# A layer with a mixer and a mixture of experts on one core: a tenth preloaded weight piece in the place of the residual's permuted copy, a strided first gather, and an end shared by ScalarE and VectorE

## The chip, the core and the metric

The kernel runs on one core of one Trainium2 chip. The metric is the device time of one execution in microseconds (us). Three runs of the kernel before have a median of 1313.36 us (1310.47 to 1313.62). The profile is of one further execution, which took 1310.38 us.

## What is computed

One layer over 256 tokens of width 2048, all in float32. First the mixer: an input projection, three token mixers, an output projection, and the residual sum. Then the experts:

```
x = x + y @ w_out                       # y: what the mixers give
h2 = rmsnorm(x, norm_ffn)
x = x + hierarchical_moe(h2, ...)       # 32 experts, 2 for each token
# in an expert:
hid = silu(xb @ w_gate[e]) * (xb @ w_up[e])     # 2048 -> 512
out = hid @ w_down[e]                           # 512 -> 2048
```

Every expert has weights of 12 MB (w_gate, w_up, w_down of 4 MB each), so the second part reads 384 MB from memory.

## The kernel before, in words

**Mixer part.** 29 weight pieces of 2 MB (21 of w_in, 8 of w_out) come through four ring buffers. ScalarE (L676) and VectorE (L989) split each into two parts, TensorE multiplies them (L1465, L1467). The last eight pieces give, in column blocks of 256, the residual sum `x_acc` (VectorE L1075, L1076), which the experts' part reads and adds to. After each block GpSimd copies it into `x2_perm` (L605, L606), in which the 128 elements that one matmul needs lie side by side; in `x_acc` they lie 16 elements (64 bytes) apart. Then come the router and the ranks of the tokens (VectorE L1202 to L1252), in which TensorE runs empty matmuls (`keep_clock`, L1407).

**Experts' part.** An expert is an item, four items are a quad, and there are eight quads. For a quad, `gather` (L1651 to L1665) multiplies the residual by a matrix of zeros and scaled ones: the residual's 128x128 chunk is the stationary operand, `pick` the moving one. There are 16 chunks for each of two token tiles, so 32 matmuls; in the first quad the first 16 stand ahead of the first item and the other 16 after its first two pieces. VectorE puts the result into `x_exp` (L1327). An item then takes its weights in six pieces of 2 MB: in the first quad in the order gate half, up half, gate half, up half (L1697), down half, down half (L1743). In between the gate and the up sums are folded over four row groups (`fold_part`, L1677: stationary `gate_sb` or `up_sb`, read 4 elements or 16 bytes apart; moving `fold`, 32 columns). After each piece TensorE raises `piece_used`. The results of an item are added to the residual while the next item runs: TensorE spreads them over the tokens (`combine`, L1647), VectorE adds (`accumulate`, L1337).

**The queue of weights.** SP issues all loads in one order. It waits for a buffer to be free, then issues. In the first quad it has eight ring buffers and one more, `starter`, for piece 8 (pieces are numbered 0 to 23 in the quad). So pieces 0 to 8 are issued with no regard to the experts' work: 0 and 1 once `y_parts` is split (`y_split`), 2 to 5 as the mixer's buffers come free (`lo_ready`), 6 to 8 as the mixer's last matmuls end (`quarter_used`). Piece 9 waits for the use of piece 0, piece 10 for that of piece 1, and so on (L451):

```
else:
    sp.wait_ge(piece_used, m - STARTER if m <= STARTER + MOE_RING else m - MOE_RING + 1)
```

From the second quad on, the same buffers are four pairs of 4 MB (`twin`), filled with a whole w_gate, w_up or w_down (L475), and the last two matrices of the last item come in halves again (L471).

**The end.** The last item has empty matmuls at two places, three ahead of the first down half and six ahead of the second (`keep_clock`). Then `combine` spreads its result: four matmuls for token tile 0 into four PSUM banks, four for tile 1 into the same banks, each of which waits until VectorE has read its bank. VectorE adds eight blocks of 512 columns (L1337), and SP writes each to memory as it is ready (L504, 256 KB each).

Of the kernel before, what the change touches and what calls it, by code (L numbers as in the profile page):

```python
# [23 lines left out]
F32 = mybir.dt.float32  # L24
# [13 lines left out]
def hymba_layer(nc, x, norm_mix, w_in, conv_a_w, conv_a_b, lru_wa, lru_ba, lru_wx, lru_bx, lru_lam,  # L38
# [54 lines left out]
    with ExitStack() as ctx:  # L93
# [43 lines left out]
        proj = at("proj", [BLK_V, SEQ], F32, o)  # L137
        x2_perm = at("x2_perm", [TILES, KC, P], F32, o)
# [79 lines left out]
        b_gath, b_up_fold, b_comb = [bank[4], bank[5]], bank[4], bank[4:8]  # L218

# [4 lines left out]
        starter_in = sem("starter_in")  # L224
# [40 lines left out]
        comb_full, acc_done = sem("comb_full"), sem("acc_done")  # L265
# [10 lines left out]
        STARTER = MOE_RING  # L276

        def slot_of(m):

            return m if m <= STARTER else (m - STARTER - 1) % MOE_RING  # L280

# [4 lines left out]
        def begun(m):  # L286
            return m == STARTER

# [16 lines left out]
        def half_landed(q, k, part, h):  # L305
# [5 lines left out]
            return q * (16 * PER_QUAD // MOE_RING) + 16 * ((3 * k + part) // (MOE_RING // 2) + 1  # L311
# [9 lines left out]
        def half_of(q, k, part, h):  # L321

            if first_quad(q):
                m = first_piece(k, part, h)
                return starter[:, :] if begun(m) else ring[MOE_ORDER[slot_of(m)]][:, :]
# [14 lines left out]

        def second_quad(q):
            return isinstance(q, int) and q == 1
# [42 lines left out]
        def _(sp):  # L385
# [48 lines left out]
            def quad(q, n_extra=None):  # L434
                def item_pieces(k, e):
                    for i in range(PARTS):
                        m = PARTS * k + i
                        if m < 2:
# [15 lines left out]
                        dst = starter if begun(m) else ring[place_of(k, i)]  # L454
                        sp.dma_start(dst[:, :].rearrange("p (c n) -> p c n", n=src.shape[2]),
                                     src).then_inc(starter_in if begun(m) else piece_in[place_of(k, i)], 16)

                def item_twins(k, e):
                    for part, whole in enumerate((w_gate_p, w_up_p, w_down_p)):
# [29 lines left out]
            quad(1)  # L489
            with sp.Fori(2, QUADS - 1) as q:  # L490
                quad(q)
# [17 lines left out]
        def _(pool):  # L509
# [91 lines left out]

            for k in range(N_OUT):
                pool.wait_ge(proj_free, N_IN + k + 1)
# [8 lines left out]
        def _(act):  # L612
# [289 lines left out]
            quad(QUADS - 1)  # L902
            act.wait_ge(table_ready, 1)
# [8 lines left out]
        def _(dve):  # L912
# [482 lines left out]
            with dve.If(n_extra > 0):  # L1395
                with dve.Fori(QUADS, QUADS + XQ) as q:
# [400 lines left out]
```

## Time and profile before

| | before |
|---|---|
| median of 3 runs | 1313.36 us (1310.47 to 1313.62) |
| profiled execution | 1310.38 us |
| its span | 1308.6 us |
| TensorE busy | 1129.7 us, 86% |
| VectorE busy | 510.0 us, 39% |
| ScalarE busy | 280.5 us, 21% |
| GpSimd busy | 57.3 us, 4% |
| read from memory | 468.83 MB |
| written to memory | 2.10 MB |

The span is the time from the first to the last recorded instruction; 1.8 us of the execution lie around it. Busy shares are means over stages with different limits. The mixer lasts until about 380 us, the router until 392, the experts until the end.

### The profile page before, as it was taken

What the parts mean: (1) busy time and instruction counts of PE and PEld (TensorE: products, weight loads), DVE (VectorE), ACT (ScalarE), POOL (GpSimd) and SP (SyncE); (2) the same over time, 40 slices, a digit from 0 to 9 for tenths busy, and PEclk for the clock granted to TensorE, in tenths of its full rate; (3) what the DMA queues carried; (4) which work ended last, traced back from release to release, by engine and by line L of the source; (5) the groups of instructions that cost most, each with busy time, mean ns of one, the idle gap of its engine ahead of it and who ended that gap; (6) DMA issues with size and microseconds to landing.
All of it is one profiled execution on the core that took longest, in us unless ns stands there. A gap on an engine that the chain in (4) does not pass through costs nothing.

```text
span 1308.6 us, 17772 instructions
## 1 busy us (share of the span) xinstructions
PE 1129.7 (86%) x7343; PEld 658.1 (50%) x7343; DVE 510.0 (39%) x817; ACT 280.5 (21%) x444; POOL 57.3 (4%) x72
## 2 busy tenths in 40 slices
PE   8999999999999988878787887987887797779677
PEld 7888888878885444324323323423242253234223
DVE  6646677775444353223222222322232232222223
ACT  7445576684430000000000000000000000000000
POOL 3000011501100000000000000000000000000000
PEclk9999999999999888888878978888788798888888
DMA  9955554746678999999999999999999999999996
GB/s 323 293 190 176 159 181 140 246 129 201 273 297 336 425 435 429 430 432 430 432 433 432 432 431 430 433 433 433 432 432 433 431 431 433 433 433 430 431 424 262
DMA packets 83856, 471.61 MB, mean 360 GB/s; under 512 B 7154, under 2 KB 68192, under 8 KB 69216
## 3 DMA queue, kind: packets, MB, share of 16 engines
q1 hardware_dynamic: 83808, 470.94, 88.2%
q8 instruction: 34, 0.56, 0.2%
q14 instruction: 14, 0.11, 0.0%
HBM read 468.83 MB, written 2.10 MB: 360 GB/s over the span
## 4 chain that ended last, share of the span: by engine, by line
PE 52%; DMA 40%; DVE 4%; ACT 1%; issue 1%; POOL 1%; DVEq 0%; SPq 0%; ACTq 0%
PE banks L1465 16%; DMA twin<-in_w_gate 15%; DMA twin<-in_w_up 15%; DMA twin<-in_w_down 10%; PE banks L1697 9%; PE banks L1467 8%; PE banks L1743 6%; PE banks L1677 3%; PE banks L1647 3%; PE banks L1663 3%; DVE x_acc L1337 2%; PE banks L1407 1%; PE banks L1486 1%; DVE up_sb L1350 1%; POOL h_tok L555 1%
## 5 line engine op out<-in xcount | busy, mean ns | idle before, releaser
L1697 PE MATMUL banks<-twin,x_exp 128*32 128x512 f32 x1760 | 252.5, 698 | 83.2 <-DMA twin<-in_w_gate 68.0
L1337 DVE TENSOR_TENSOR x_acc<-x_acc,banks 128x512 f32<-128x512 f32 x256 | 158.5, 682 | 343.5 <-PE banks L1647 343.4
L1465 PE MATMUL banks<-hT,w_split 128*128 128x512 f32 x576 | 203.9, 398 | 0.1
L989 DVE TENSOR_TENSOR w_split<-ring,w_split 128x1024 fp32r<-128x1024 f32 x116 | 146.7, 1284 | 112.6 <-ACT w_split L676 112.0
L1697 PEld LDWEIGHTS banks<-twin,x_exp 128*32 128x32 f32 x1760 | 50.0, 118 | 236.2 <-issue 131.7
L1467 PE MATMUL banks<-hT,w_split 128*128 128x256 f32 x576 | 161.2, 280 | 0.0
L1743 PE MATMUL banks<-twin,hidT 128*32 128x512 f32 x864 | 144.3, 829 | 19.3 <-DVE hidT L1356 9.7
L676 ACT ACTIVATE w_split<-ring 128x1024 fp32r<-128x1024 f32 x116 | 121.7, 1060 | 122.0 <-PE banks L1467 121.9
L1465 PEld LDWEIGHTS banks<-hT,w_split 128*128 128x128 f32 x576 | 108.0, 188 | 25.4 <-issue 0.3
L888 ACT ACTIVATE y_item<-banks 64x512 f32<-64x512 f32 x32 | 18.9, 591 | 472.4 <-PE banks L1743 472.4
L1467 PEld LDWEIGHTS banks<-hT,w_split 128*128 128x128 f32 x576 | 108.7, 189 | 0.2
L1677 PE MATMUL banks<-fold,up_sb 128*128 128x32 f32 x256 | 65.5, 399 | 42.4 <-DVE up_sb L1350 42.4
L1677 PEld LDWEIGHTS banks<-fold,up_sb 128*128 128x128 f32 x256 | 62.2, 327 | 72.2 <-DVE x_acc L1337 55.4
L1647 PE MATMUL banks<-y_item,give 32*128 32x512 f32 x512 | 93.8, 769 | 2.6 <-DVE x_acc L1337 1.8
L1361 DVE COPY y_item<-banks 64x512 f32<-64x512 f32 x32 | 22.2, 695 | 179.3 <-PE banks L1743 179.3
L1465 PE MATMUL banks<-w_split,y_parts 128*128 128x512 f32 x256 | 90.6, 398 | 0.5 <-DVE y_parts L1058 0.5
L1743 PEld LDWEIGHTS banks<-twin,hidT 128*32 128x32 f32 x864 | 34.6, 144 | 107.1 <-issue 92.8
L872 ACT ACTIVATE gate_sb<-banks 128x512 f32<-128x512 f32 x32 | 19.1, 597 | 305.1 <-PE banks L1697 305.1
L1677 PE MATMUL banks<-fold,gate_sb 128*128 128x32 f32 x256 | 65.7, 401 | 8.2 <-ACT gate_sb L872 8.2
L1467 PE MATMUL banks<-w_split,y_parts 128*128 128x256 f32 x256 | 71.4, 279 | 0.0
L1677 PEld LDWEIGHTS banks<-fold,gate_sb 128*128 128x128 f32 x256 | 62.1, 327 | 16.5 <-ACT gate_sb L872 15.9
L1647 PEld LDWEIGHTS banks<-y_item,give 32*128 32x128 f32 x512 | 27.4, 229 | 83.4 <-issue 79.1
(244 smaller groups left out, 925.9 us busy)
## 6 DMA issues: line engine op xcount, KB each, us to landing
twin<-in_w_gate SPq DMA_DIRECT2D x28, 4096.0 KB, 32.5
twin<-in_w_up SPq DMA_DIRECT2D x27, 4096.0 KB, 32.3
twin<-in_w_down SPq DMA_DIRECT2D x27, 4096.0 KB, 32.3
ring<-in_w_in SPq DMA_DIRECT2D x20, 2048.0 KB, 9.0
ring<-in_w_up SPq DMA_DIRECT2D x10, 2048.0 KB, 15.8
ring<-in_w_down SPq DMA_DIRECT2D x10, 2048.0 KB, 16.7
ring<-in_w_out SPq DMA_DIRECT2D x8, 2048.0 KB, 8.3
ring<-in_w_gate SPq DMA_DIRECT2D x7, 2048.0 KB, 11.8
```

Source lines behind the costliest of these rows:

```text
L676: act.activation(w_hi[:, k], src, ACT.Copy).then_inc(hi_ready, 1)
L872: act.activation(gate_sb[:, :], b_gate[:, :], ACT.Copy).then_inc(gate_out, 1)
L989: dve.tensor_tensor(w_lo[:, k], src, w_hi[:, k].bitcast(F32), ALU.subtract).then_inc(lo_ready, 1)
L1337: dve.tensor_tensor(dst, dst, b_comb[n][:, :], ALU.add).then_inc(acc_done, 1)
L1361: dve.tensor_copy(y_item[k % 2][P // 2:P, :], b_down[P // 2:P, :]).then_inc(y_out_dve, 1)
L1465: pe.matmul(dst[:, 0:2 * PW], stationary[:, 0, cols], moving.rearrange("p s n -> p (s n)"), start=(k == 0 and cc == 0), stop=False)
L1467: ins = pe.matmul(dst[:, PW:2 * PW], stationary[:, 1, cols], moving[:, 0, :], start=False, stop=(k == 3 and cc == 3))
L1647: pe.matmul(b_comb[n][:, :], give[par][rows, t, :], y_item[par][rows, :], start=True, stop=True).then_inc(comb_full, 1)
L1663: ins = pe.matmul(b_gath[b % 2][:, c * P:(c + 1) * P], x2_perm[:, t, 4 * b + c, :], pick[:, t].rearrange("p i s -> p (i s)"), start=(t == ...
L1677: ins = pe.matmul(to[:, f * SLOTS:(f + 1) * SLOTS], part[:, :].rearrange("p (k f) -> p f k", f=FC)[:, f, :], fold[:, :], start=True, stop= ...
L1697: ins = pe.matmul(dst[SLOTS * j:SLOTS * (j + 1), :], x_exp[:, c, cols], weights[:, cc * F:(cc + 1) * F], start=(c < 4), stop=(c >= KC - 4))
L1743: ins = pe.matmul(b_down[SLOTS * n:SLOTS * (n + 1), :], hidT[:, f, :], weights[:, ff * D + n * DB:ff * D + (n + 1) * DB], start=(f == 0), ...
```

## The change

- `starter2`, a buffer of 2 MB, is laid over `x2_perm`. It takes piece 2 of the first quad (the second gate half of the first expert), and SP issues it with pieces 0 and 1. The ring buffer that piece 2 had goes to piece 3, and so on, so that piece 9 has a buffer of its own, too. Pieces 0 to 9 are now issued ahead, and pieces 10 to 23 wait for `piece_used`.
- `x2_perm` can only be written when piece 2 has been used. GpSimd now makes its 16 copies then, in one go. VectorE waits for them ahead of its first addition to `x_acc`, and the second quad's gather waits for them.
- The first quad's gather reads `x_acc` itself, with its chunks' elements 64 bytes apart.
- SP's second quad is no longer written out; its waits follow the rule of the later ones.
- At the end, the empty matmuls give way to four matmuls that put blocks 1 and 3 of each token tile of the residual into PSUM (`residual_first`, stationary `ident`, 512 moving columns). The last combine uses eight banks and waits for none to be read; for blocks 1 and 3 it adds to what is there, and ScalarE copies the sum out. VectorE adds blocks 0 and 2 as before. The output goes in four writes of 512 KB, each after one addition and one copy.
- VectorE raises `acc_done` four times more where there are further items, which is a branch that this input doesn't take (no instruction of it is in the trace).

```diff
+        starter2 = at("starter2", [KC * PW], F32, o)
...
+        last_comb = [bank[4:8], [bank[3], bank[0], bank[1], bank[2]]]
...
-        STARTER = MOE_RING
+        STARTERS = (8, 2)
+        FIRST = MOE_RING + len(STARTERS)
         def slot_of(m):
-            return m if m <= STARTER else (m - STARTER - 1) % MOE_RING
+            if m >= FIRST:
+                return (m - FIRST) % MOE_RING
+            return m - len([e for e in STARTERS if e < m])
...
-        def slot_user(s):
-
-            return max(m for m in range(PER_QUAD) if not begun(m) and slot_of(m) == s)
+        def slot_user(s, upto=PER_QUAD):
+
+            return max(m for m in range(upto) if not begun(m) and slot_of(m) == s)
+
+        FIRST_PAIR = (PER_QUAD - FIRST) % MOE_RING // 2
         def twin_of(k, part):
-            return (3 * k + part) % (MOE_RING // 2)
+            return (3 * k + part + FIRST_PAIR) % (MOE_RING // 2)
...
+                        if m < 2 or begun(m) and begun_at(m) == 1:
                             sp.wait_ge(y_split, 4)
-                        elif m < 6:
-
-                            sp.wait_ge(lo_ready, 4 * (N_MIX - 6 + m) + 4)
-                        elif m == 6:
-
-                            sp.wait_ge(quarter_used, 4 * N_MIX - 2)
-                        elif m <= STARTER:
+                        elif begun(m):
                             sp.wait_ge(quarter_used, 4 * N_MIX)
+                        elif slot_of(m) < 6 and m < FIRST:
+
+                            sp.wait_ge(lo_ready, 4 * (N_MIX - 6 + slot_of(m)) + 4)
+                        elif m < FIRST:
+
+                            sp.wait_ge(quarter_used, 4 * N_MIX - 2 if slot_of(m) == 6 else 4 * N_MIX)
                         else:
-                            sp.wait_ge(piece_used, m - STARTER if m <= STARTER + MOE_RING else m - MOE_RING + 1)
+                            sp.wait_ge(piece_used, slot_user(slot_of(m), m) + 1)
...
-                        if second_quad(q) and 3 * k + part < 4:
-
-                            sp.wait_ge(piece_used, max(slot_user(2 * j), slot_user(2 * j + 1)) + 1)
-                        else:
-                            sp.wait_ge(piece_used, q * PER_QUAD + 2 * (3 * k + part) - 6)
+                        sp.wait_ge(piece_used, q * PER_QUAD + 2 * (3 * k + part) - 6)
...
-            quad(1)
-            with sp.Fori(2, QUADS - 1) as q:
+            with sp.Fori(1, QUADS - 1) as q:
...
-            for b in range(8):
-                t, n = b // 4, b % 4
+            for b in range(4):
+                t, d = b // 2, slice(b % 2 * 2 * DB, (b % 2 + 1) * 2 * DB)
                 sp.wait_ge(acc_done, (NE - 1) * 8 + (b + 1))
-                sp.dma_start(out_t[t][:, n * DB:(n + 1) * DB], x_acc[:, t, n * DB:(n + 1) * DB]).then_inc(out_done, 16)
-            sp.wait_ge(out_done, 16 * 8)
+                sp.wait_ge(acc_done_act, b + 1)
+                sp.dma_start(out_t[t][:, d], x_acc[:, t, d]).then_inc(out_done, 16)
+            sp.wait_ge(out_done, 16 * 4)
...
+            pool.wait_ge(piece_used, STARTERS[1] + 1)
             for k in range(N_OUT):
-                pool.wait_ge(proj_free, N_IN + k + 1)
...
             quad(QUADS - 1)
+
+            for b in range(4):
+                t, n = b // 2, b % 2 * 2 + 1
+                act.wait_ge(comb_full, (NE - 1) * 8 + (4 * t + n + 1))
+                act.activation(x_acc[:, t, n * DB:(n + 1) * DB], last_comb[t][n][:, :],
+                               ACT.Copy).then_inc(acc_done_act, 1)
...
+                if first_quad(q) and k == 1:
+
+                    dve.wait_ge(x2_perm_ready, N_OUT)
...
-            accumulate(NE - 1, 0)
-            accumulate(NE - 1, 1)
+            for b in range(4):
+                t, n = b // 2, b % 2 * 2
+                dve.wait_ge(comb_full, (NE - 1) * 8 + (4 * t + n + 1))
+                dst = x_acc[:, t, n * DB:(n + 1) * DB]
+                dve.tensor_tensor(dst, dst, last_comb[t][n][:, :], ALU.add).then_inc(acc_done, 1)
...
+            def residual_first(t, n):
+
+                pe.matmul(last_comb[t][n][:, :], ident[:, :], x_acc[:, t, n * DB:(n + 1) * DB], start=True, stop=False)
+
+            def last_combine(t):
+
+                outputs_written(NE)
+                pe.wait_ge(give_ready, NE)
+                for n in range(4):
+                    rows = slice(SLOTS * n, SLOTS * (n + 1))
+                    pe.matmul(last_comb[t][n][:, :], give[1][rows, t, :], y_item[1][rows, :],
+                              start=(n % 2 == 0), stop=True).then_inc(comb_full, 1)
...
-                if first_quad(q):
-                    pe.wait_ge(x2_perm_ready, N_OUT)
+                def x2_chunk(t, c):
+                    if first_quad(q):
+                        return x_acc[:, t, :].rearrange("p (k c) -> p c k", c=KC)[:, c, :]
+                    return x2_perm[:, t, c, :]
+
                 pe.wait_ge(pick_ready, q + 1)
                 if not first_quad(q):
+
+                    pe.wait_ge(x2_perm_ready, N_OUT)
...
-                            ins = pe.matmul(b_gath[b % 2][:, c * P:(c + 1) * P], x2_perm[:, t, 4 * b + c, :],
+                            ins = pe.matmul(b_gath[b % 2][:, c * P:(c + 1) * P], x2_chunk(t, 4 * b + c),
...
-                    keep_clock(b_up, 3)
+
+                    pe.wait_ge(acc_done, (NE - 1) * 8)
+                    for n in (1, 3):
+                        residual_first(0, n)
...
-                        keep_clock(b_up, 6)
+
+                        pe.wait_ge(give_ready, NE)
+                        for n in (1, 3):
+                            residual_first(1, n)
...
-            combine(NE - 1, 0, 1)
-            combine(NE - 1, 1, 1)
+            last_combine(0)
+            last_combine(1)
```

On the queue SP, in the first quad, the program before had these loads (the ring's number is behind the name; one row for each piece, from piece 0):

```order
L455 DMA ring6_56<-in_w_gate 128x4096 [waits y_split]
L455 DMA ring7_57<-in_w_up 128x4096 [waits y_split]
L455 DMA ring1_51<-in_w_gate 128x4096 [waits lo_ready]
L455 DMA ring2_52<-in_w_up 128x4096 [waits lo_ready]
L455 DMA ring3_53<-in_w_down 128x4096 [waits lo_ready]
L455 DMA ring0_50<-in_w_down 128x4096 [waits lo_ready]
L455 DMA ring4_54<-in_w_gate 128x4096 [waits quarter_used]
L455 DMA ring5_55<-in_w_up 128x4096 [waits quarter_used]
L455 DMA starter_76<-in_w_gate 128x4096 [waits quarter_used]
L455 DMA ring6_56<-in_w_up 128x4096 [waits piece_used]
```

and the changed one has these:

```order
L463 DMA ring6_56<-in_w_gate 128x4096 [waits y_split]
L463 DMA ring7_57<-in_w_up 128x4096 [waits y_split]
L463 DMA starter2_82<-in_w_gate 128x4096 [waits y_split]
L463 DMA ring1_51<-in_w_up 128x4096 [waits lo_ready]
L463 DMA ring2_52<-in_w_down 128x4096 [waits lo_ready]
L463 DMA ring3_53<-in_w_down 128x4096 [waits lo_ready]
L463 DMA ring0_50<-in_w_gate 128x4096 [waits lo_ready]
L463 DMA ring4_54<-in_w_up 128x4096 [waits quarter_used]
L463 DMA starter_76<-in_w_gate 128x4096 [waits quarter_used]
L463 DMA ring5_55<-in_w_up 128x4096 [waits quarter_used]
L463 DMA ring6_56<-in_w_down 128x4096 [waits piece_used]
```

Ten loads instead of nine stand ahead of the first that waits for the experts' work. Piece 2 moved from the third wait for `lo_ready` to that for `y_split`, and each of pieces 3 to 7 has taken the wait of the one before it.

On TensorE, from the last item's second fold to its last combine, the program before had (`y_item_77` and `give_78` are the last item's result and its table of gates):

```order
L1677 MATMUL banks<-fold,up_sb 128x32 x3
L1407 MATMUL banks<-ident 128x128 x3
L1743 MATMUL banks<-ring_54,hidT 32x512 [waits y_out_dve,piece_in4,y_out_act,hid_ready]
L1743 MATMUL banks<-ring_54,hidT 32x512 x7
L1407 MATMUL banks<-ident 128x128 x6
L1743 MATMUL banks<-ring_55,hidT 32x512 [waits piece_in5]
L1743 MATMUL banks<-ring_55,hidT 32x512 x7
L1647 MATMUL banks<-y_item_77,give_78 128x512 [waits give_ready,acc_done,y_out_dve,y_out_act]
L1647 MATMUL banks<-y_item_77,give_78 128x512 [waits acc_done] x3
```

and the changed one:

```order
L1715 MATMUL banks<-fold,up_sb 128x32 x3
L1659 MATMUL banks<-x_acc,ident 128x512 [waits acc_done]
L1659 MATMUL banks<-x_acc,ident 128x512
L1787 MATMUL banks<-ring_53,hidT 32x512 [waits y_out_dve,piece_in3,y_out_act,hid_ready]
L1787 MATMUL banks<-ring_53,hidT 32x512 x7
L1659 MATMUL banks<-x_acc,ident 128x512 [waits give_ready]
L1659 MATMUL banks<-x_acc,ident 128x512
L1787 MATMUL banks<-ring_50,hidT 32x512 [waits piece_in0]
L1787 MATMUL banks<-ring_50,hidT 32x512 x7
L1667 MATMUL banks<-y_item_77,give_78 128x512 [waits give_ready,y_out_dve,y_out_act]
L1667 MATMUL banks<-y_item_77,give_78 128x512 x3
```

Two wide matmuls stand where three narrow ones stood, and two where six stood, both ahead of a down half; the combine's wait for `acc_done` is gone.

## Rows read from the trace of the kernel before

**Rows 1.** The page: traffic in 40 equal slices, and the chain's shares.
```profile
GB/s 323 293 190 176 159 181 140 246 129 201 273 297 336 425 435 429 430 432 430 432 433 432 432 431 430 433 433 433 432 432 433 431 431 433 433 433 430 431 424 262
PE 52%; DMA 40%; DVE 4%; ACT 1%; issue 1%; POOL 1%; DVEq 0%; SPq 0%; ACTq 0%
```

**Rows 2.** Stretches: us, busy by engine (count), TensorE clock, DMA share, GB/s.
```profile
345.00:370.00 25.00, 25.00 (x148) 21.06 (x147) 12.75 (x13) 11.52 (x20) 2.29 (x4) 1.00 0.46 172
393.50:399.00 5.50, 5.50 (x53) 3.49 (x55) 1.65 (x4) 0.00 (x0) 0.00 (x0) 1.00 0.00 0
399.00:401.00 2.00, 2.00 (x21) 1.16 (x14) 0.00 (x0) 0.00 (x0) 0.00 (x0) 1.00 0.89 246
```

**Rows 3.** Timeline of SP's queue: start, us, instruction.
```profile
319.86 1.82 SPq L455 DMA_DIRECT2D ring<-in_w_gate  x1
...
379.26 0.43 SPq L455 DMA_DIRECT2D starter<-in_w_gate  x1
398.38 0.33 SPq L455 DMA_DIRECT2D ring<-in_w_up  x1
400.09 5.95 SPq L455 DMA_DIRECT2D ring<-in_w_down  x2
410.34 0.33 SPq L455 DMA_DIRECT2D ring<-in_w_gate  x1
415.58 0.33 SPq L455 DMA_DIRECT2D ring<-in_w_up  x1
417.30 0.33 SPq L455 DMA_DIRECT2D ring<-in_w_gate  x1
```

**Rows 4.** The chain in order of time, the first item: start, us, what.
```profile
392.89 3.57 PE banks L1663 x32
396.46 3.57 PE banks L1697 x32
400.03 3.77 PE banks L1663 x32
403.80 1.90 PE banks L1697 x16
```

**Rows 5.** Timeline: weight loads with contiguous, strided and contiguous stationary operands.
```profile
383.64 0.52 PEld L1606 LDWEIGHTS banks<-fold_halves,logitsT 128*128 128x128 f32 x4 [1.42 <-DVE logitsT L1157]
406.37 1.94 PEld L1677 LDWEIGHTS banks<-fold,gate_sb 128*128 128x128 f32 x8 [0.55 <-ACT gate_sb L872]
399.96 3.65 PEld L1663 LDWEIGHTS banks<-pick,x_perm 128*128 128x128 f32 x32 [0.84 <-issue]
```

**Rows 6.** Timeline: GpSimd's last pair of copies, and VectorE's first additions.
```profile
380.37 1.12 POOL L606 COPY x_perm<-x_acc 128x256 f32<-128x256 f32 x2 [8.94 <-DVE x_acc L1076]
422.76 4.87 DVE L1337 TENSOR_TENSOR x_acc<-x_acc,banks 128x512 f32<-128x512 f32 x8
```

**Rows 7.** The chain in order of time, the last item: start, us, what.
```profile
1240.22 33.50 DMA twin<-in_w_gate
1291.16 0.75 PE banks L1407 x6
1293.77 1.54 PE banks L1407 x12
1295.30 1.90 PE banks L1743 x16
```

**Rows 8.** Stretches at the end, columns as in group 2.
```profile
1300.50:1306.25 5.75, 2.37 (x8) 0.86 (x6) 3.52 (x6) 0.00 (x0) 0.00 (x0) 0.68 0.98 360
1306.25:1308.60 2.35, 0.00 (x0) 0.00 (x0) 0.00 (x0) 0.00 (x0) 0.00 (x0) 0.50 0.09 29
```

**Rows 9.** Timeline of the end: the last additions and the output's writes.
```profile
1299.15 4.87 DVE L1337 TENSOR_TENSOR x_acc<-x_acc,banks 128x512 f32<-128x512 f32 x8 [1.23 <-PE banks L1647]
1299.86 4.52 SPq L504 DMA_DIRECT2D out<-x_acc  x8
```

**Rows 10.** One line's instructions: ns min/median/max, and ScalarE's copy of 512 columns.
```profile
L872 ACT ACTIVATE gate_sb<-banks x32: 597/597/599, 405.7 to 1278.7; 128x512 f32<-128x512 f32 x32
```

More of the change, by code:

```diff
@@ L223, in hymba_layer @@
         piece_in = [sem(f"piece_in{i}") for i in range(MOE_RING)]
-        starter_in = sem("starter_in")
+        starter_in = [sem(f"starter_in{i}") for i in range(2)]
         consts_ready = sem("consts_ready")
@@ L264, in hymba_layer @@
         y_out_act, y_out_dve = sem("y_out_act"), sem("y_out_dve")
-        comb_full, acc_done = sem("comb_full"), sem("acc_done")
+        comb_full, acc_done, acc_done_act = sem("comb_full"), sem("acc_done"), sem("acc_done_act")
         gath_full, gath_out = sem("gath_full"), sem("gath_out")
@@ L286, in begun, with begun_at @@
         def begun(m):
-            return m == STARTER
+            return m in STARTERS
+        def begun_at(m):
+            return STARTERS.index(m)
         def uses_of(m):
             return len([e for e in range(m + 1) if not begun(e) and slot_of(e) == slot_of(m)])
-        def slot_user(s):
-            return max(m for m in range(PER_QUAD) if not begun(m) and slot_of(m) == s)
+        def slot_user(s, upto=PER_QUAD):
+            return max(m for m in range(upto) if not begun(m) and slot_of(m) == s)
+        FIRST_PAIR = (PER_QUAD - FIRST) % MOE_RING // 2
         def twin_of(k, part):
-            return (3 * k + part) % (MOE_RING // 2)
+            return (3 * k + part + FIRST_PAIR) % (MOE_RING // 2)
         def half_place(q, k, part, h):
@@ L310, in half_landed @@
                 return 16 * (uses_of(slot_user(s)) + 1 + MIX_USES[half_place(q, k, part, h)])
-            return q * (16 * PER_QUAD // MOE_RING) + 16 * ((3 * k + part) // (MOE_RING // 2) + 1
+            in_first = uses_of(slot_user(2 * twin_of(k, part))) - PER_QUAD // MOE_RING
+            return q * (16 * PER_QUAD // MOE_RING) + 16 * ((3 * k + part) // (MOE_RING // 2) + 1 + in_first
                                                            + MIX_USES[half_place(q, k, part, h)])
@@ L324, in half_of @@
                 m = first_piece(k, part, h)
-                return starter[:, :] if begun(m) else ring[MOE_ORDER[slot_of(m)]][:, :]
+                return (starter, starter2)[begun_at(m)][:, :] if begun(m) else ring[MOE_ORDER[slot_of(m)]][:, :]
             if apart(q, k, part):
@@ L339, in first_quad @@
             return isinstance(q, int) and q == 0
-        def second_quad(q):
-            return isinstance(q, int) and q == 1
         def closing_quad(q):
@@ L437, in item_pieces @@
                         m = PARTS * k + i
-                        if m < 2:
+                        if m < 2 or begun(m) and begun_at(m) == 1:
                             sp.wait_ge(y_split, 4)
-                        elif m < 6:
-                            sp.wait_ge(lo_ready, 4 * (N_MIX - 6 + m) + 4)
-                        elif m == 6:
-                            sp.wait_ge(quarter_used, 4 * N_MIX - 2)
-                        elif m <= STARTER:
+                        elif begun(m):
                             sp.wait_ge(quarter_used, 4 * N_MIX)
+                        elif slot_of(m) < 6 and m < FIRST:
+                            sp.wait_ge(lo_ready, 4 * (N_MIX - 6 + slot_of(m)) + 4)
+                        elif m < FIRST:
+                            sp.wait_ge(quarter_used, 4 * N_MIX - 2 if slot_of(m) == 6 else 4 * N_MIX)
                         else:
-                            sp.wait_ge(piece_used, m - STARTER if m <= STARTER + MOE_RING else m - MOE_RING + 1)
+                            sp.wait_ge(piece_used, slot_user(slot_of(m), m) + 1)
                         src = piece_source(i, e)
-                        dst = starter if begun(m) else ring[place_of(k, i)]
+                        dst = (starter, starter2)[begun_at(m)] if begun(m) else ring[place_of(k, i)]
                         sp.dma_start(dst[:, :].rearrange("p (c n) -> p c n", n=src.shape[2]),
-                                     src).then_inc(starter_in if begun(m) else piece_in[place_of(k, i)], 16)
+                                     src).then_inc(starter_in[begun_at(m)] if begun(m) else piece_in[place_of(k, i)], 16)
                 def item_twins(k, e):
@@ L1391, in _ @@
             quad(QUADS - 1)
-            accumulate(NE - 1, 0)
-            accumulate(NE - 1, 1)
+            for b in range(4):
[3 more added lines that the diff above has]
+                dve.tensor_tensor(dst, dst, last_comb[t][n][:, :], ALU.add).then_inc(acc_done, 1)
             n_extra = dve.value_load(tab[0:1, 0:1], min_val=0, max_val=NX - 1)
             with dve.If(n_extra > 0):
+                dve.wait_ge(acc_done_act, 4)
+                for b in range(4):
+                    dve.tensor_copy(lru_t[:, 0, b:b + 1], silu_sb[:, 0, 0:1]).then_inc(acc_done, 1)
                 with dve.Fori(QUADS, QUADS + XQ) as q:
@@ L1630, in landed @@
                     if begun(m):
-                        pe.wait_ge(starter_in, 16)
+                        pe.wait_ge(starter_in[begun_at(m)], 16)
                     else:
```

## The prediction

> **What bounds the kernel.** I began with the traffic over the whole span [rows 1]. From slice 15 to slice 39 it stands at 424 to 435 GB/s and never lower: once the experts run, the weights' stream is the bound. The last number, 262, and the numbers up to the 14th are lower: there something else holds the transfers back. The chain's shares say the same: 40% of it is DMA, and TensorE's 52% is mostly the mixer and the ends of items. So three places matter: when the stream starts without a hole, how many pieces it has left then, and what lies behind its last pieces.
>
> The start is seen in the stretches [rows 2]: nothing moves from 393.5 to 399.0 us, because all nine preloaded pieces have landed and the tenth waits for the first to be used. From 399 to 401 the queue moves 246 GB/s x 2 us = 0.49 MB, which at 431 GB/s takes 1.14 us, so the stream starts at about 399.86. SP issued at 398.38 [rows 3], so from issue to stream is 1.48 us. A piece of 2.097 MB takes 4.86 us at 431 GB/s. The chain in that time is TensorE alone: gather 3.57 us, two pieces 3.57, gather 3.77, third piece 1.90 [rows 4].
>
> **What the tenth piece gives.** One piece less is left at the start: at most 4.86 us. Loading it ahead costs nothing: SP issues it behind pieces 0 and 1, at about 322, 1.9 us and a load after the one at 319.86 [rows 3], and between 345 and 370 the DMA engines are idle 54% of the time [rows 2], 13.5 us. The mixer's last w_out piece was issued before them, so it isn't delayed.
>
> But less of it arrives. Before, the refills were issued when pieces 0 to 4 had been used: 398.38, 400.09, 405.71 (second of the pair at 400.09), 410.34, 415.58, then 417.30 [rows 3]. The stream needed them at 399.86 + 4.86 each: the third refill at 409.58, the fourth at 414.44, the fifth at 419.30. In the change the second gate half has no buffer to give back (its place becomes `x2_perm`), so the third refill waits for the fourth use: 410.34 + 1.48 = 411.82 instead of 409.58. The fourth waits for the fifth use: 415.58 + 1.48 = 417.06, where the stream is ready at 411.82 + 4.86 = 416.68. Before, this same data started at 419.30. With all else equal the stream is 2.2 us earlier, not 4.86. The later refills aren't late (417.30 + 1.48 against 421.92).
>
> **What the strided gather costs.** The first gather's stationary operand is now read with 64 bytes between elements. No row shows that stride, but one shows 16 bytes: the fold's eight loads of 128x128 take 1.94 us, 0.243 each [rows 5]. With the same number of partitions and 36 moving columns in place of 32, but a contiguous operand, four take 0.52 us, 0.130 each; the gather's own 32 take 3.65, 0.114 each [rows 5]. So a stride costs 0.113 to 0.129 us for a load; I take 0.12. A half of the gather has 32 loads (two for each float32 matmul): 3.8 us more. TensorE is the chain here [rows 4] and nothing covers it. Bounds: nothing extra if the fold were slow for another reason, and twice as much, 0.24 us, since 64 bytes are further than 16; I take the fold's value, because its elements too lie each in another 16 bytes.
>
> The Trainium skill (SBUF — State Buffer, Door 1, on SBUF cachelines) says that accesses within a 16-byte line run at full bandwidth and each crossing pays, and also that four fp32 are free to stride. The fold, at just four, pays, so the trace bears out the first half and not the second. By the first, 64 bytes would cost what 16 do.
>
> Uses 0 and 1 come 3.8 us later, use 3 and all after it 7.6. The fourth refill then starts at 415.58 + 7.6 + 1.48 = 424.66 (the third at 410.34 + 9.08 = 419.42, done at 424.28). Against 419.30 the stream is **5.4 us later**. The fifth, at 417.30 + 9.08 = 426.4, is in time for 429.5. From there on SP is ahead of the stream, and its one-piece-earlier waits in the second quad change nothing.
>
> **The copies on GpSimd.** They were behind other work before, so removing them from the mixer saves nothing. Now 16 of them start after use 2, at 405.71 + 7.6 = 413.3, and take 16 x 0.56 = 9 us at the pace of the last pair [rows 6], until 422.3. VectorE would wait for them at its first addition, 422.76 + 7.6 = 430.4 [rows 6]. Cover: 8 us; cost nothing. Without that cover, the second item's combine and fold would wait behind VectorE.
>
> **The end.** The last item hangs on its gate matrix, which lands at 1273.7 [rows 7]; from there TensorE, VectorE and ScalarE follow each other without another wait for a load. Three empty matmuls took 0.75 us and six 1.54 [rows 7]. A full-width pass of 512 columns costs what four quarter-width ones side by side do: 16 in 1.90 us [rows 7], four rounds, so 0.43 to 0.48 each, and two passes for each float32 matmul: 0.86 to 0.95. Two matmuls are 1.7 to 1.9 us. Both groups stand ahead of a down half, so the last down half ends 1.0 + 0.2 = 1.2 us later.
>
> Behind it, VectorE's eight additions took 4.87 us from 1299.15 to 1304.02 [rows 9]. Four remain, beside four copies of 0.60 on ScalarE [rows 10]: 2.5 us. This alone ends the arithmetic 2.4 - 1.2 = 1.2 us earlier. But the writes don't follow it: from 1300.5 to 1306.25 the DMA engines are 98% busy with the output's 2.1 MB at 360 GB/s, and 2.35 us of tail come behind [rows 8]. The first write needs one addition, as before, now 1.2 us later (before: 1299.86 [rows 9]). So the end comes 1.2 us later, unless rows of 4 KB in place of 2 KB move faster; at 431 GB/s they would win 0.9. I take **+0.8 us**, with bounds of -1.2 (the last addition sets the end) and +1.2.
>
> **Sum.** 5.4 + 0.8 = +6.2 us on the profiled execution's 1310.4: 1316.6. The median of the runs shown, 1313.4, is 3.0 us above that execution, so I say **1319.6 us**, 0.5% slower than the median. About 0.3% (3.9 us) is what a measurement of this kernel can tell from no change.
>
> **Rivals.**
> 1. *The strided loads cost nothing.* The fold might be slow for its many small outputs. For it: no row has this stride. Against it: the four loads with 36 columns write small outputs as well [rows 5]. Then the stream gains 2.2 us, and the end gives -1.2 to +1.2: 1310.0 to 1312.4, not slower. What decides is the pace of the gather: the gain of 2.2 us is used up at 0.035 us more for each of the 64 loads, that is at 0.149 us a load against 0.114.
> 2. *The tenth piece decides.* The full 4.86 us come through because transfers that were issued late are made good. Against it: a bound stream can't catch up, the plateau is flat [rows 1]. With free loads and the arithmetic setting the end it would be 1313.4 - 4.9 - 1.2 = 1307.3.
> 3. *64 bytes cost twice what 16 do, or TensorE's clock falls to its lower level in the first item* while it waits on loads. 7.6 us more, or about 2 us for each piece in it: 1323 to 1327.
> 4. *The copies aren't covered.* If they took over 1.06 us each (17 us in all), VectorE would wait and TensorE's combine behind it; at 1.5 us each 7 us, most of which the loads queued by then would hide: at the worst a third of it, 1322.
>
> **How the numbers follow.** Forecast 0.60; rival 1 0.19; rival 2 0.06; rival 3 0.12; rival 4 0.03. In the forecast the time can be as low as 1317 if the median lies nearer to the fast execution, and its own range is 1316 to 1321.5. The range of 1310.0 to 1323.5 takes in rival 1 and the lower part of rival 3. Slower by over 0.3% (over 1317.3): most of the forecast, 0.53, and rivals 3 and 4, together 0.68. Faster by over 0.3% (under 1309.4): rival 2 and a corner of rival 1, 0.07. Within: 0.25.
>
> **What would show it.** Right: the first quad's two halves of the gather take about 7.5 us each in place of 3.7; SP's first refill is issued at about 402.2, the third at 418, the fourth at 423; a hole of some 6 us in the traffic between them; GpSimd's copies end near 422 with VectorE not waiting; the last down half ends 1.2 us later relative to the gate's landing; the output moves for 5 us or more after the first write. Wrong: gather loads at 0.11 us, or a third refill at 410 (rival 1); a stream that reaches its last piece earlier than before; a write phase that shrinks with the additions.

## The result, and the profile after

| | before | changed |
|---|---|---|
| median of 9 runs | 1311.38 us (1309.2 to 1313.92) | 1318.67 us (1316.81 to 1322.12) |
| ratio | 1 | 1.0053, 95% interval 1.0044 to 1.0062 |
| span of the profiled execution | 1308.6 us | 1315.5 us |

The changed kernel is slower by 7.0 us (5.8 to 8.1); 6.2 had been forecast. One of the twelve executions of the new end alone (experiment 1) took 2426 us at a granted clock of 0.42 and is in no ratio here. The traffic of the changed kernel, in the same 40 slices as in [rows 1]:

```profile
GB/s 322 292 189 182 159 173 151 233 128 222 341 270 262 426 436 430 429 430 433 430 430 431 431 431 432 431 433 431 433 431 431 431 431 431 430 431 431 431 427 208
```

The plateau is the same. The tenth piece is in the 11th slice (341 for 273), the loss in the 13th (262 for 336) and in the last. SP's queue, to be read against [rows 3]:

```profile
322.46 0.44 SPq L463 DMA_DIRECT2D starter<-in_w_gate  x1
...
400.02 2.04 SPq L463 DMA_DIRECT2D ring<-in_w_down  x2
415.40 0.33 SPq L463 DMA_DIRECT2D ring<-in_w_gate  x1
420.64 0.33 SPq L463 DMA_DIRECT2D ring<-in_w_up  x1
422.36 0.33 SPq L463 DMA_DIRECT2D ring<-in_w_gate  x1
```

After the first two refills comes a pause of 13.7 us in which only 9.7 us of transfers are queued. By the prediction's account the stream then lacks a load from 411.22 (400.02 + 1.48 + 2 x 4.86) to 416.88 (415.40 + 1.48), 5.7 us for the 6 forecast. The stretches show the hole:

```profile
402.00:405.00 3.00, 3.00 (x16) 3.00 (x15) 0.00 (x0) 0.00 (x0) 0.00 (x0) 1.00 0.98 415
...
412.00:414.00 2.00, 2.00 (x15) 1.66 (x18) 0.00 (x0) 0.47 (x2) 2.00 (x5) 1.00 0.00 0
414.00:416.00 2.00, 1.34 (x16) 0.13 (x5) 0.59 (x1) 0.08 (x1) 2.00 (x5) 1.00 0.00 0
```

The cause is in the chain. The halves of the gather take 6.99 and 7.18 us, for 3.57 and 3.77 in [rows 4]; all else in the item is as it was:

```profile
391.12 6.99 PE banks L1701 x32
398.11 3.57 PE banks L1735 x32
401.68 7.18 PE banks L1701 x32
408.86 1.90 PE banks L1735 x16
```

The same line's weight loads, by what they read (ns min/median/max). The first row is the later quads, from the permuted copy, the second the first quad:

```profile
L1701 PEld LDWEIGHTS banks<-pick,x_perm x448: 186/192/338, 490.5 to 1192.4; 128*128 128x128 f32 x150
...
L1701 PEld LDWEIGHTS banks<-pick,x_acc x64: 291/312/313, 390.9 to 408.4; 128*128 128x128 f32 x64
```

GpSimd's copies are where they were expected, and nobody waits for them; VectorE first adds to `x_acc` at 427.83, 9 us after they end:

```profile
410.81 7.90 POOL L610 COPY x_perm<-x_acc 128x256 f32<-128x256 f32 x16 [126.74 <-PE banks L1735]
```

At the end, the chain from the last gate matrix on, against [rows 7]:

```profile
1244.45 32.80 DMA twin<-in_w_gate
...
1277.29 3.35 PE banks L1735 x16
...
1296.12 1.80 PE banks L1659 x4
1297.92 1.85 PE banks L1787 x16
1299.77 1.91 PE banks L1659 x4
1301.69 1.90 PE banks L1787 x16
1303.59 0.02 issue
```

The two pairs of wide matmuls take 1.80 and 1.91 us where the empty ones took 0.75 and 1.54. The 6.9 us between the spans split so:

| | before | changed | difference |
|---|---|---|---|
| last gate matrix landed | 1273.72 | 1277.25 | +3.5 |
| from there to the end of the last down half | 23.5 | 26.3 | +2.9 |
| from there to the end of the span | 11.4 | 11.9 | +0.5 |

Of the 2.9 us, 1.4 are the wide matmuls. The other 1.4 are the first gate half, 3.35 us for 1.92: the granted clock is 0.60 there (1277 to 1281), which moves about from execution to execution (below).

The arithmetic behind the last down half did get shorter, as forecast: from its end to that of the last addition it takes 4.4 us (1303.59 to 1308.01) where it took 6.8 (1297.20 to 1304.02). The end of the span didn't follow it, as forecast too.

### The profile page after: what moved, and what is told of

It reads as the page before. It is cut to its first block, busy times and chain, and to the rows that moved or that the text cites. A ratio compares the mean times of both kernels' runs of the same rounds, so it can differ in the third digit from the quotient of the medians.

```text
span 1315.5 us, 17791 instructions
## 1 busy us (share of the span) xinstructions
PE 1135.1 (86%) x7333; PEld 662.2 (50%) x7333; DVE 507.6 (39%) x813; ACT 282.6 (21%) x448; POOL 56.1 (4%) x72
## 4 chain that ended last, share of the span: by engine, by line
PE 52%; DMA 40%; DVE 4%; ACT 1%; issue 1%; POOL 0%; DVEq 0%; SPq 0%; POOLq 0%; ACTq 0%
DMA twin<-in_w_up 18%; PE banks L1485 16%; DMA twin<-in_w_gate 15%; PE banks L1735 9%; PE banks L1487 8%; DMA twin<-in_w_down 7%; PE banks L1787 6%; PE banks L1715 3%; PE banks L1701 3%; PE banks L1680 3%; DVE x_acc L1347 1%; PE banks L1427 1%; PE banks L1506 1%; DVE up_sb L1363 1%; PE banks L1538 0%
## 5 line engine op out<-in xcount | busy, mean ns | idle before, releaser
L1735 PE MATMUL banks<-twin,x_exp 128*32 128x512 f32 x1760 | 255.8, 707 | 83.7 <-DMA twin<-in_w_gate 64.3
L1347 DVE TENSOR_TENSOR x_acc<-x_acc,banks 128x512 f32<-128x512 f32 x248 | 153.6, 683 | 344.5 <-PE banks L1680 344.4
L1787 PE MATMUL banks<-twin,hidT 128*32 128x512 f32 x864 | 143.1, 823 | 18.1 <-DVE hidT L1369 11.4
L1680 PE MATMUL banks<-y_item,give 32*128 32x512 f32 x496 | 88.3, 761 | 1.0 <-DVE x_acc L1347 1.0
```

The costliest lines, as they stand in the source:

```text
L1347: dve.tensor_tensor(dst, dst, b_comb[n][:, :], ALU.add).then_inc(acc_done, 1)
L1680: pe.matmul(b_comb[n][:, :], give[par][rows, t, :], y_item[par][rows, :], start=True, stop=True).then_inc(comb_full, 1)
L1735: ins = pe.matmul(dst[SLOTS * j:SLOTS * (j + 1), :], x_exp[:, c, cols], weights[:, cc * F:(cc + 1) * F], start=(c < 4), stop=(c >= KC - 4))
L1787: ins = pe.matmul(b_down[SLOTS * n:SLOTS * (n + 1), :], hidT[:, f, :], weights[:, ff * D + n * DB:ff * D + (n + 1) * DB], start=(f == 0), ...
```

## The experiments

All were timed in five rounds against the kernel before, but for the one on strides. A ratio of 1.0010 is 1.3 us.

**1. The new end alone** (`e2`): the parts of the diff on `last_comb`, `residual_first`, `last_combine`, on ScalarE's copies and on the four writes, on the kernel before.

> The kernel before with the new end alone (four wide matmuls for nine empty ones, additions and copies shared, four writes of 512 KB). Theory: the four wide matmuls take 3.7 us in the changed kernel where the empty ones took 2.3, so TensorE ends 1.4 us later, and the writes take 0.5 us more from the first issue to the end: +1.9 us, ratio 1.0014. Rival (the shared end pays, and the whole loss is the gather's): -1.2 us, ratio 0.999. The first item's gather must stay at 3.6 to 3.8 us a half.

Measured 1.0012 (1.0003 to 1.0021), +1.6 us. The new end loses by itself, and the rival is out. Its chain shows the wide matmuls again, 2.47 us (partly at the lower clock) and 1.91:

```profile
1291.26 2.47 PE banks L1652 x4
1293.73 2.83 PE banks L1775 x16
1296.56 1.91 PE banks L1652 x4
1298.47 1.90 PE banks L1775 x16
```

**2. The strided gather alone** (`e3`). The line of the edit that counts; `x2_chunk` (not shown) takes the chunk from `x_acc` in the first quad and from `x2_perm` later.

```diff
-                            ins = pe.matmul(b_gath[b % 2][:, c * P:(c + 1) * P], x2_perm[:, t, 4 * b + c, :],
+                            ins = pe.matmul(b_gath[b % 2][:, c * P:(c + 1) * P], x2_chunk(t, 4 * b + c),
```

> The kernel before, in which only the first quad's gather reads the residual itself with 64 bytes between elements; the permuted copy is made as before and is used from the second quad on. Theory: each half of the gather takes 3.4 us more, the use of the fourth and fifth piece comes 6.8 us later, and the stream passes from 2.2 us ahead of its refills to 4.6 us behind: the fifth refill starts at 415.58 + 6.84 + 1.48 = 423.9 in place of 419.3, +4.6 us, ratio 1.0035. Rival (the queue makes up for late refills): under +1 us.

Measured 1.0051 (1.0037 to 1.0065), +6.7 us: nearly the whole loss comes from this one edit. The 4.6 that I expected lies just under the interval (4.9 to 8.5); it holds only where the item runs without a low time of the clock (see "Two errors that cancelled in part"). In the trace the use of piece 4 comes at 422.53, as worked out (422.42), though for two reasons that cancel: the first use came 1.3 us earlier, and the item took 1.4 us more, since the low time of the clock (0.63 from 420 to 424) fell into it. The load that waits for it starts 4.7 us later than before (424.01 for 419.30). The three stretches of 2 us from 422 on, at 303, 311 and 369 GB/s, lack 1.4 us of traffic; that is the hole itself, from 422.50, when the load ahead is through, to 424.01. The reads of weights then run out 4.9 us later than before, at about 1295.8 for 1290.9 (estimates, from 336 and 74 GB/s in the two stretches of 4 us from 1292 on, and 287 and 29 from 1288 on before, at 431 GB/s). But the last gate matrix landed 7.0 us later (1280.68 for 1273.72). The 2 us that the start doesn't explain thus lie at the landing of this one matrix; why stays open.

**3. The changed kernel with the old end** (`e4`).

> The changed kernel with the old end: tenth piece, later copies, strided gather. Theory: the fifth use sets the start of the same refill with nine pieces and with ten, so the tenth piece gives nothing at all once the gather is strided: +4.6 us, ratio 1.0035, the same as the strided gather alone within 0.5 us. Rival (the tenth piece gives its 4.86 us whatever the gather costs): about 0, ratio 1.000. Second rival (the copies on GpSimd delay VectorE): more than the strided gather alone by 1 us or more.

Measured 1.0055 (1.0041 to 1.0070), +7.2 us: the same as the strided gather alone, 0.5 us apart, as the theory allowed, with intervals of about 2 us on either side. So, as far as these can tell, with a strided gather the tenth piece is worth nothing; a gain of 4.86 us is excluded. Its trace shows why: the load that waits for piece 4 starts at 427.27, set by that use (425.79 + 1.48), while the loads ahead of it were through at 425.37. A delay of 1 us by GpSimd's copies can't be excluded by these times; in the changed kernel's trace nobody waits for them.

**4. The tenth piece without the stride's cost** (`e5`: old end, contiguous chunks).

```diff
-                        return x_acc[:, t, :].rearrange("p (k c) -> p c k", c=KC)[:, c, :]
+                        return x_acc[:, t, c * P:(c + 1) * P]
```

> As the kernel with the tenth piece and the old end, but the first quad's gather reads 128 elements side by side from the residual, which are other elements than the layer needs, so this part of the computation is changed. It shows the tenth piece without the cost of the stride. Theory: the refill after the second piece waits for the fourth use, so of 4.86 us only 2.2 come through: -2.2 us, ratio 0.9983. Rival (all of it comes through): -4.9 us, ratio 0.9963.

Measured 0.9995 (0.9987 to 1.0004), -0.6 us. The rival of -4.9 is excluded, but my -2.2 lies outside as well. The queue says why:

```profile
397.11 2.04 SPq L463 DMA_DIRECT2D ring<-in_w_down  x2
409.07 0.33 SPq L463 DMA_DIRECT2D ring<-in_w_gate  x1
415.13 0.33 SPq L463 DMA_DIRECT2D ring<-in_w_up  x1
```

From the first to the fifth use it takes 18.0 us; in the profile before it took 415.58 - 398.38 = 17.2, at full clock. With ten pieces the fifth use sets the stream's start directly, so each such delay is paid; with nine there are 2.2 us of room for it. The gain was worked out from an execution in which the item ran without a low time. A full 2.2 us of delay in the item would use it up.

**5. The changed kernel whole, but with contiguous chunks** (`e1`: the edit of 4 on the changed kernel).

> The changed kernel whole, but the first quad's gather reads 128 elements side by side (other elements than the layer needs, so this part of the computation is changed). Theory: what the tenth piece alone showed, -0.6 us, plus what the new end alone showed, +1.6: +1.0 us, ratio 1.0008, so that the stride accounts for some 6 of the 7 us. Rival (parts of the change other than the stride cost as much together as it does): +3 us or more.

Measured 1.0008 (0.9996 to 1.0020), +1.0 us. The parts add up: -0.6 for the tenth piece, +1.6 for the end; the rival of +3 or more lies outside. The stride is the other 6 of the 7.

**6. Four strides in one gather** (`e6`, one profiled execution).

```diff
-                        return x_acc[:, t, :].rearrange("p (k c) -> p c k", c=KC)[:, c, :]
+                        s = 2 << (c // 4)
+                        return x_acc[:, t, 0:s * P].rearrange("p (k c) -> p c k", c=s)[:, c % s, :]
```

> The changed kernel, in which the four blocks of the first quad's gather read their stationary chunks from the residual with 2, 4, 8 and 16 elements (8, 16, 32 and 64 bytes) from one to the next, so the first quad's items compute with other elements. 16 loads for each stride. Theory: what costs is that an element lies in another 16 bytes than the one before: 16, 32 and 64 bytes take the same 0.22 us a load, 8 bytes take 0.11 to 0.12. Rival (the cost grows with the distance): 16 bytes well under 0.22, 32 between, 64 the most.

The line's loads in the stretches of the four strides; columns as above. The first row is 8 bytes (with one load of the next), then 16 (12 of its 16 loads), 32 and 64:

```profile
L1702 PEld LDWEIGHTS banks<-pick,x_acc x17: 196/196/311, 391.5 to 393.4; 128*128 128x128 f32 x17
...
L1702 PEld LDWEIGHTS banks<-pick,x_acc x12: 329/329/329, 394.3 to 396.9; 128*128 128x128 f32 x12
...
L1702 PEld LDWEIGHTS banks<-pick,x_acc x16: 313/335/336, 400.9 to 404.5; 128*128 128x128 f32 x16
...
L1702 PEld LDWEIGHTS banks<-pick,x_acc x16: 310/312/315, 404.7 to 408.0; 128*128 128x128 f32 x16
```

8 bytes cost nothing beside a contiguous read (196 ns against 192), 16, 32 and 64 bytes cost alike (329, 335, 312). The fold's 256 loads, at 16 bytes in the kernel before, take 327 ns in the mean as well. It is a step and not a slope: the rival falls. The theory holds in its numbers, but its wording asks for more care: at 8 bytes every second element lies in another 16 bytes than the one before, and that costs nothing. The cost comes where every element does. By starts, 16 loads take 1.9 us at 8 bytes and 3.7, 3.8 and 3.4 at the others.

**7. A late fifth use alone** (`e12`), on the kernel before.

```diff
+                if begins:
+                    keep_clock(b_up, 20)
                 pe.wait_ge(hid_ready, i + 1)
```

> The kernel before with 20 empty matmuls (4.66 us, 0.5 of them hidden behind a wait that is there anyway) in the first item, between the fourth and the fifth use. Nothing else is moved, and the first four refills keep their times. Theory: only what is late beyond the slack of 2.2 us reaches the end: 4.2 - 2.2 = +2.0 us, ratio 1.0015, up to +3.5 where the clock's low time falls into the item and has used the slack up. Rival (no slack: every late microsecond in the first item counts): +4.2. Rival (the queue makes up for it): 0.

Measured 1.0026 (1.0016 to 1.0036), +3.4 us. The rival of 0 is out. Between the other two the times don't decide: the +2.0 lies just under the interval (2.1 to 4.7), which holds the +3.5 of an item with a low time and the 4.2 as well. The trace does. The fourth use is at 408.35, the fifth at 417.62, 9.3 us later where it was 5.2 [rows 3], so 4.0 us late:

```profile
408.35 0.33 SPq L455 DMA_DIRECT2D ring<-in_w_gate  x1
417.62 0.33 SPq L455 DMA_DIRECT2D ring<-in_w_up  x1
```

and a hole of under 2 us opens behind it:

```profile
412.00:416.00 4.00, 4.00 (x38) 3.67 (x40) 0.00 (x0) 0.00 (x0) 0.00 (x0) 1.00 1.03 442
416.00:420.00 4.00, 4.00 (x44) 1.22 (x40) 0.66 (x1) 0.59 (x1) 0.00 (x0) 1.00 0.77 262
420.00:424.00 4.00, 4.00 (x40) 1.07 (x36) 3.59 (x14) 0.00 (x0) 0.00 (x0) 1.00 0.95 401
```

262 GB/s for 4 us lacks 1.6 us of traffic and 401 another 0.3: of the 4.0 us, 1.9 reach the stream. In this execution the slack of 2.2 is there.

**8. Writes of 512 KB alone** (`e8`): SP's four writes on the kernel before, each after two additions.

> The kernel before with four writes of 512 KB in place of eight of 256 KB; each waits for two additions. Theory: the first write is issued 0.61 us later, and the second is held up on its queue as in the changed kernel (1.5 us in issue), which leaves a gap in the traffic: +1 us, ratio 1.0008. Rival (rows of 4 KB move faster and win it back): -0.3 to 0 us.

Measured 1.0002 (0.9993 to 1.0010): no difference that can be told. Neither my +1 us nor the rival's gain is shown. But this run doesn't have what I had priced: its four writes took 0.33 to 0.35 us each on SP's queue, so none was held up. It shows that the size alone makes no difference that can be told, and leaves the hold-up of the changed kernel unpriced.

**9. Without the six empty matmuls at the end** (`e7`).

> The kernel before without the six empty matmuls ahead of the last down half. Theory: the last piece has landed at about 1293.0 and TensorE starts on it at 1295.30, behind 1.54 us of empty matmuls that stand on the chain: -1.5 us, ratio 0.9989. Rival (they keep the clock up, and without them the last combine and additions run at the lower level): 0 to +1 us.

Measured 0.9990 (0.9980 to 1.0000), -1.3 us, for -1.5 expected; no difference at all is the edge of its interval. The profile before flattered the end: there the first down half took 1.9 us, while in other executions with the old end it took 3.0 to 3.5. Without the six, both halves together take 5.1 to 5.3:

```profile
1294.65 5.14 PE banks L1743 x32
```

**10. Gaps filled ahead of the router** (`e10`).

> The kernel before with 2, 2 and 4 more empty matmuls in the three gaps (0.5, 0.4 and 1.0 us) in which TensorE waits between the last mixer piece and the router. In the executions seen, the clock is at its lower level for a time either in the router's empty matmuls (the ranks then come 1.6 us later) or in the first two items (the fourth use then comes up to 1.5 us later). Theory: it falls because of the gaps ahead of the router; with them filled the rank matmuls start at 388.5 to 389.1 and the fifth refill earlier, -1.5 us, ratio 0.9989, and less spread. Rival (the low time comes from elsewhere and is only moved): 0.

Measured 0.9991 (0.9981 to 1.0000), -1.2 us, again at the edge. That it works as the theory says is not shown. The low time came in this execution, too, only in the first item (clock 0.64):

```profile
384.00:388.00 4.00, 4.00 (x39) 4.00 (x38) 3.11 (x19) 0.75 (x3) 0.00 (x0) 1.00 1.02 426
412.00:416.00 4.00, 3.77 (x24) 1.10 (x28) 0.17 (x1) 0.00 (x0) 0.00 (x0) 0.64 1.01 434
```

**11. Both together** (`e11`): the kernel before without the six, with the 2, 2 and 4.

> The kernel before without the six empty matmuls at the end and with the 2, 2 and 4 ahead of the router. Alone they gave -1.3 and -1.2 us, each at the edge of its interval. Theory: they lie at the two ends of the stream and add: -2.5 us, ratio 0.9981. Rival (one or both were chance): -1 us or less. It would be the fastest of all kernels here.

Measured 0.9984 (0.9973 to 0.9995), -2.1 us, median 1309.33 (1308.5 to 1312.09, 12 runs). Its median is the lowest here, but its interval overlaps with those of the other two (0.9990 and 0.9991), so that it is faster than either is not shown. The effects add within their intervals; the rival of -1 us or less is not quite excluded (-3.5 to -0.7).

## Why the prediction was right

**Number and mechanism.** The loss came from where it was expected: the strided gather delays the use that sets the stream's start, the tenth piece then gives nothing back, and the new end adds a little. The time of 1319.6 was nearer to the measured 1318.67 than the working deserves: the change cost 0.8 us more than forecast, and the kernel before ran at 1311.4 in these rounds and not at the 1313.4 that I started from.

**The account of the stream held.** The prediction said that the start of one load, the one that waits for the use of piece 4 (piece 13 in both kernels), sets all that follows. Its start is the later of the use + 1.48 us and the end of the loads ahead of it, at 4.86 us each. Worked out in this way from each trace's queue, and set against the landing of the last gate matrix:

| trace | first use | use of piece 4 | start of that load | last gate landed | between |
|---|---|---|---|---|---|
| before | 398.38 | 415.58 | 419.30 | 1273.72 | 854.4 |
| changed | 400.02 | 420.64 | 422.12 | 1277.25 | 855.1 |
| end alone | 397.85 | 417.61 | 419.09 | 1273.88 | 854.8 |
| stride alone | 400.55 | 422.53 | 424.01 | 1280.68 | 856.7 |
| old end | 402.10 | 425.79 | 427.27 | 1282.21 | 854.9 |
| tenth alone | 397.11 | 415.13 | 416.61 | 1271.23 | 854.6 |
| late fifth | 396.39 | 417.62 | 419.10 | 1274.36 | 855.3 |
| gaps filled | 397.01 | 415.06 | 417.93 | 1272.28 | 854.4 |

850 us later, the difference is the same to within 1 us, but for the stride alone. The five traces that are not in the table (`e1`, `e6`, `e7`, `e8`, `e11`) give 854.3 to 854.9 as well. What happens to this load in the first item is neither lost nor made good until the end.

**The strided gather.** Forecast from the fold at 16 bytes: 3.8 us for each half; measured 3.42 and 3.41. A load was 0.22 us apart from the next, and not 0.23 to 0.24. I had weighed two sentences of the Trainium skill (SBUF — State Buffer, Door 1, on SBUF cachelines). The rule of the 16-byte line stands there with a condition that I had left out, at least two hits in each line. With it experiment 6 agrees: a step of two elements has two hits in each line and costs nothing, a step of four has one and pays. Without it, each crossing would pay, and two elements would cost something. Its remark that one can stride over four fp32 for free, read as a step of four, is contradicted: four cost as much as sixteen.

**The tenth piece.** Loading it ahead was free, as said: from 370.0 to 393.5 the two traces move 355 and 351 GB/s, and the load that ends the preloading is issued at 379.26 and 379.09. That 2.2 us of its 4.86 come through was right for the execution it was worked out from and too much on average: 0.6 (-0.5 to 1.7).

**The copies on GpSimd** took 7.9 us (9 forecast) and ended at 418.7, 9 us ahead of VectorE's need (8 forecast). Right.

**The rivals.** The loads' pace of 0.22 us rules out the first, experiment 3 the second, the copies' 7.9 us the fourth. Of the third, the first half is out (64 bytes cost what 16 do); the second, a low time of the clock in the first item, didn't come in the changed kernel's trace, but in those of the stride alone and of the old end, where the item took 1.4 and 3.1 us more.

**The end.** Wide matmuls: +1.2 forecast, +1.4 measured. The writes: I had the end follow the first write, which came 1.2 us later, and took 0.4 off for rows of 4 KB. In the trace there is nothing to take off: from the first write to the end of the span it takes 9.2 us for 8.7. A gap in the traffic accounts for about 0.3 of it, by its 147 GB/s:

```profile
1307.50:1308.00 0.50, 0.00 (x0) 0.00 (x0) 0.50 (x1) 0.14 (x1) 0.00 (x0) 1.00 1.04 401
...
1308.50:1309.00 0.50, 0.00 (x0) 0.00 (x0) 0.00 (x0) 0.00 (x0) 0.00 (x0) 1.00 0.42 147
1309.00:1309.50 0.50, 0.00 (x0) 0.00 (x0) 0.00 (x0) 0.00 (x0) 0.00 (x0) 1.00 1.05 418
```

In sum the end alone is +1.6 (0.4 to 2.8) for a forecast of +0.8; the term was sized too small, and its upper bound of +1.2 lies inside the interval.

**Two errors that cancelled in part.** The use of piece 4 was forecast for 423.2 in the changed kernel and came at 420.64. Of these 2.5 us, 0.8 are the stride's smaller cost, and 1.8 lie ahead of the gather: the first use in the profile before came late. Its router's 20 empty matmuls ran partly at the lower clock (0.57 from 384 to 388) and took 6.34 us, in the changed kernel's trace 4.71. The clock of that one execution was thus 1.6 us of the two traces' difference and nothing of the change. So the start of the load moved by 2.8 us in the traces and not by 5.4, and the landing of the last gate matrix by 3.5.

On the other side the profile before ran its first item at full clock and its end with less time at the lower one, which made the stream's slack look larger and the end shorter than they mostly are. From the first use to that of piece 4 it takes 17.2 us there. In eleven traces (all but those of the four strides and of the late fifth use; the strided ones less the gather's 3.4) it is 17.2 to 20.3. With nine pieces and contiguous chunks such a delay is free up to 2.2 us; with the strided gather, and with the tenth piece, all of it is paid. Over these eleven the part of the slack that is used up has a mean of 1.1 us. By the prediction's own account, then, the strided gather costs 4.6 + 1.1 = 5.7 us on average and the tenth piece gives 2.2 - 1.1 = 1.1; both are estimates, and both lie in their measured intervals, as 4.6 and 2.2 don't. With the strided gather's 5.7, nothing for the tenth piece and the end's 1.6 the whole change comes to 7.3, for the measured 7.0. For the end: from the landing of the last gate matrix to the end of the span it is 34.9 us in the profile before, 36.5 to 37.7 in the five other traces with the old end whole, and 36.8 to 38.3 in the four with the new one.

One reading was off without effect: the plateau of the traffic starts in the 14th slice (425) and not in the 15th.

## What to carry to other kernels

When a queue refills buffers as they are used, work out for each early refill how long before the stream needs it the use comes; the smallest of these is what a further buffer could give here, and the most that the code in front may be slowed for free. A buffer that can't be refilled helps only before the first refill. A float32 stationary operand that is read in steps costs nothing extra here at a step of two elements, and twice the spacing between loads from four on, so a permuted copy can halve the time of a gather that its loads pace (7.0 us for 3.6). And look at the same row in several executions before a microsecond of it is put into a sum.

## What the runs showed of the hardware that had not been expected

- **The stride's step** (experiment 6): 128x128 float32 weight loads take 192 ns contiguous, 196 at 8 bytes, 329, 335 and 312 at 16, 32 and 64. From four elements on, the distance makes no further difference.
- **The lower clock moves about.** Eleven of the thirteen traces, all but the changed kernel's and that of the late fifth use, have a time of some 4 us or more between 384 and 425 with a granted clock well under 1.00, near the lower of its two levels (1.2 GHz): in the router for the kernel before (0.57 from 384 to 388), in the first item for most others (0.57 from 408 to 412 with the end alone, 0.64 from 412 to 416 with the gaps filled), in both for two. Where it falls in the router, the stream starts 1.6 us later; where it falls in the first item, that takes 0.6 to 3.1 us more. This fits the spread of 1309 to 1314 us, though no run ties the two. What makes it fall at the one place or the other stays open.
- **A write that was held in issue.** The changed kernel's second write of 512 KB took 1.51 us on SP's queue, where writes of 256 KB took 0.33:

```profile
1306.85 1.51 SPq L508 DMA_DIRECT2D out<-x_acc  x1
```

The gap in the traffic at 1308.5 follows it. The other three traces with the new end show it as well, with 1.11 to 1.38 us for the second write. In experiment 8, with writes of the same size that are issued 1.2 us or more apart and not 0.6, none was held. So the size alone doesn't bring it about; what does, and what it costs, no run shows.
